# A hybrid encoder layer with routed experts: where the closing part loads its rows, and how the router's logits are multiplied

## What is computed

```python
def layer(...):
    h = rms_norm(x) * (1 + sc1) + sh1
    mix, ... = token_mixer(h, ...)            # gated short conv and windowed attention, merged, times w_mix_out
    x = x + g1 * mix                          # the kernel's "x2"
    h = rms_norm(x) * (1 + sc2) + sh2         # the kernel's "h2"
    top_idx, top_w = route(hf, w_router, router_bias)
    ffn = swiglu(hf, w_sh_gate, w_sh_up, w_sh_down) + routed_experts(hf, top_idx, top_w, ...)
    x = x + g2 * ffn
    return x                                  # then one last RMSNorm with a gain

def route(h, w_router, router_bias):
    scores = sigmoid(h @ w_router)            # (tokens, 64 experts), contraction over 1024
    # best 4 of 8 groups, best 8 experts in them, weights normalised and times 2.5
```

## Time and profile before

| | |
|---|---|
| median of the runs | 2250.11 us |
| profiled execution | 2247.8 us |
| its span | 2246.0 us |
| granted TensorE clock, mean | 0.979 of full speed |
| TensorE matmul busy | 2140.7 us (95%) |
| VectorE busy | 1230.8 us (55%) |
| ScalarE busy | 1007.1 us (45%) |
| GpSimd busy | 459.5 us (20%) |

### The profile page before, as it was taken

The page is one execution under the profiler, slowest core; times in us unless marked ns, Lnnn a source line. Parts: engine busy times, 40 slices in busy tenths (PEclk is TensorE's granted clock), DMA queues, the critical chain, the costliest instruction groups (busy, mean ns, idle before and its releaser), DMA issues. The chain is left out here.

```text
span 2246.0 us, 41415 instructions
## 1 busy us (share of the span) xinstructions
PE 2140.7 (95%) x11538; PEld 1834.9 (82%) x11539; DVE 1230.8 (55%) x2000; ACT 1007.1 (45%) x1773; POOL 459.5 (20%) x549
## 2 busy tenths in 40 slices
PE   5999899999999989998988999999999999999995
PEld 2767559999999989997878788888888888888862
DVE  4623673112332331215777787688677778678636
ACT  3403793211011121113432676677676677667622
POOL 1400000000000000000000444434444444434335
PEclk8999899999999999999999999999999999999998
DMA  7360501112111101116322899899889899989758
GB/s 294 125 241 9 177 1 56 38 47 66 47 47 40 34 19 47 47 52 233 115 64 86 295 326 312 252 304 335 278 285 340 279 325 309 312 253 324 253 133 244
DMA packets 153532, 395.59 MB, mean 176 GB/s; under 512 B 22124, under 2 KB 90932, under 8 KB 128900
## 3 DMA queue, kind: packets, MB, share of 16 engines
q1 hardware_dynamic: 122260, 311.61, 38.5%
q0 software_dynamic: 31040, 82.51, 14.9%
q10 hardware_dynamic: 176, 0.75, 0.1%
HBM read 353.93 MB, written 74.53 MB: 191 GB/s over the span
## 5 line engine op out<-in xcount | busy, mean ns | idle before, releaser
L2098 PE MATMUL ex_pgu<-ex_wgu_hi,ex_xT_hi 128*128 (+1 forms) x784 | 314.9, 402 | 9.9 <-DVE ex_xT_lo L2268 9.2
L2256 DVE TENSOR_TENSOR ex_wgu_lo<-ex_stage_gu,ex_wgu_hi (+1 forms) x252 | 291.8, 1221 | 37.2 <-ACT ex_wgu_hi L2175 37.0
L2098 PE MATMUL ex_pgu<-ex_wgu_hi,ex_xT_lo 128*128 (+1 forms) x784 | 308.1, 393 | 0.0
L2098 PE MATMUL ex_pgu<-ex_wgu_lo,ex_xT_hi 128*128 (+1 forms) x784 | 307.2, 392 | 0.0
L2175 ACT CAST ex_wgu_hi<-ex_stage_gu (+1 forms) x252 | 245.7, 1047 | 35.6 <-issue 18.7
L983 PE MATMUL cv_ph<-fourth_r,cv_split 128*128 128x352 f32 (+1 forms) x1152 | 222.0, 328 | 2.1 <-DVE cv_split L1029 2.1
L983 PEld LDWEIGHTS cv_ph<-fourth_r,cv_split 128*128 128x128 f32 x1152 | 196.0, 189 | 2.2 <-DVE cv_split L1029 2.2
L1624 POOL MEMSET ex_rows<- 128x1088 f32 x1 | 1.0, 1004 | 951.6 <-ACT third_r L1596 951.6
L2098 PEld LDWEIGHTS ex_pgu<-ex_wgu_hi,ex_xT_hi 128*128 128x128 f32 x784 | 148.4, 189 | 41.4 <-issue 11.8
L2098 PEld LDWEIGHTS ex_pgu<-ex_wgu_hi,ex_xT_lo 128*128 128x128 f32 x784 | 147.5, 188 | 31.4
L2098 PEld LDWEIGHTS ex_pgu<-ex_wgu_lo,ex_xT_hi 128*128 128x128 f32 x784 | 147.9, 189 | 28.7
(11 more groups left out here) (355 smaller groups left out, 4245.1 us busy)
## 6 DMA issues: line engine op xcount, KB each, us to landing
ex_stage_gu<-in_w_exp_gate SPq DMA_DIRECT2D x64, 1024.0 KB, 8.8
ex_stage_gu<-in_w_exp_up SPq DMA_DIRECT2D x64, 1024.0 KB, 11.7
ex_stage_dn<-in_w_exp_down SPq DMA_DIRECT2D x64, 1024.0 KB, 8.4
front_room<-in_w_ada SPq DMA_DIRECT2D x26, 512.0 KB, 5.8
w_ahead<-in_w_in SPq DMA_DIRECT2D x24, 512.0 KB, 3.8
third<-in_w_ada SPq DMA_DIRECT2D x16, 512.0 KB, 8.6
early_late<-in_w_in SPq DMA_DIRECT2D x16, 512.0 KB, 3.9
front_room<-in_w_in SPq DMA_DIRECT2D x3, 2048.0 KB, 12.6
```

Of the source, the lines that this page charges most:

```text
L2098: last = pe.matmul(pgu[:, :], xT[a][:, k, :], w, start=(k == 0 and (a, c) == PASSES[0]), stop=(k == KT - 1 and (a, c) == PASSES[-1]))
L2256: dve.tensor_tensor(gu_piece(1, slot, q), gu_raw(slot, q), gu_piece(0, slot, q).bitcast(F32), ALU.subtract).then_inc(gu_lo, 1)
```

## The change

In the closing part SP issues the eight `x2` rows one after the other, without waiting for `tail_sum`; it waits for the even scatters' own semaphore instead of `even_stored`, which is gone; and it loads the nine tiles of even sums with nothing between them.

The logits are multiplied the other way round: the router's 64 columns are the weights, the tokens are streamed. Contraction steps 0 to 3 add up in PSUM partitions 0 to 63, steps 4 to 7 in partitions 64 to 127, issued in turn. ScalarE copies the 128x128 result (experts of both halves by tokens) to SBUF, and one more matmul, with a matrix of two identities below each other (`both_halves`), adds the halves and turns them to tokens by experts. This last matmul stands in the next mix tile, behind its first two contraction steps.

```diff
-                        for k in range(KT):
-                            last = pe.matmul(pl[t % 2][:R, 0:NE], h2T[:, k, t * P:t * P + R], wr[:, k, :],
-                                             start=(k == 0), stop=(k == KT - 1))
-                        last.then_inc(lg, 1)
+                        for k in range(KT // 2):
+                            for a in range(2):
+                                j = a * (KT // 2) + k
+                                last = pe.matmul(pl[t % 2][a * NE:(a + 1) * NE, P:P + R], wr[:, j, :], h2T[:, j, t * P:t * P + R],
+                                                 start=(k == 0), stop=(k == KT // 2 - 1))
+                        last.then_inc(lg_halves, 1)
+
+                    def sum_halves(t):
+
+                        R = rows_of(t)
+                        pe.wait_ge(sum_ready, 1)
+                        pe.wait_ge(lg_out, t + 1)
+                        pe.matmul(pl[t % 2][:R, 0:NE], halves[t % 2][:, 0:R], both_halves, start=True, stop=True).then_inc(lg, 1)
...
+                            if k == 1 and t >= 3:
+                                sum_halves(t - 3)
...
+                                if half == 0 and k == 1 and q < 2:
+                                    sum_halves(NT - 2 + q)
...
                     logits(NT - 2)
+                    sum_halves(NT - 3)
                     unit(0)
...
+                    def halves_out(t):
+                        R = rows_of(t)
+                        act.wait_ge(lg_halves, t + 1)
+                        act.copy(halves[t % 2][:, 0:R], pl[t % 2][:, P:P + R]).then_inc(lg_out, 1)
...
                     for t in range(NT):
                         R = rows_of(t)
+                        if t >= 2:
+                            halves_out(t - 2)
                         act.wait_ge(x2_done, t + 1)
...
+                    dve.tensor_tensor(both_halves, con[:, C_ID:C_ID + NE], con[:, C_ID + NE:C_ID + P], ALU.add).then_inc(sum_ready, 1)
...
-                    AHEAD = 3
-                    for t in range(AHEAD):
+                    for t in range(NT - 1):
                         x2_rows(t)
-                    for t in range(AHEAD, AHEAD + 2):
-                        sp.wait_ge(tail_sum, t - AHEAD + 1)
-                        x2_rows(t)
-                    sp.wait_ge(even_stored, 1)
+                    sp.wait_ge(y_stored[0], pairs_of(sp) * 16 + 16)
                     for t in range(NT):
                         R = rows_of(t)
                         sp.dma_start(sums[t][:R, :], self.sum_rows[0][t * P:t * P + R, :]).then_inc(sum_loaded[t], 16)
-                        if AHEAD + 2 + t < NT - 1:
-                            x2_rows(AHEAD + 2 + t)
...
-                    wait(y_stored[0], m * 16 + 16)
-                    pool.sem_inc(even_stored, 1)
```

More of the change, by code:

```diff
@@ L1260, in mix_and_route @@
         sh_down_loaded = S("sh_w_down")
+        lg_halves, lg_out, sum_ready = map(S, ("mx_logit_halves", "mx_logit_halves_out", "mx_sum_of_halves"))
         sh_loaded, sh_prod, sh_sig, sh_gated, sh_done = map(S, ("sh_w", "sh_prod", "sh_sig", "sh_gated", "sh_done"))
@@ L1311, in mix_and_route @@
             wd = room(2, NE).rearrange("p (t n) -> p t n", n=NE)
+            both_halves = room(NE)
+            halves = [room(P), little(P)]
             wu_r = self.alias("sh_wu_r", [P, KT, DSH], F32R)
@@ L1596, in valued @@
                         act.activation(v, v.bitcast(F32), ACT.Copy, scale=con[:, C_VAL + t * TOPK:C_VAL + t * TOPK + 1]).then_inc(hot, 1)
+                    halves_out(NT - 2)
                     sigmoid(NT - 2)
@@ L1606, in _ @@
                     evac(NT - 1)
+                    halves_out(NT - 1)
                     sigmoid(NT - 1)
@@ L1835, in experts @@
         w_loaded = self.first_w
-        filled, ahead, even_stored = S("ex_filled"), S("cb_ahead"), S("cb_even_stored")
+        filled, ahead = S("ex_filled"), S("cb_ahead")
         x2_loaded = [S(f"cb_x2_{t}") for t in range(NT - 1)]
```

## The result

The changed kernel takes 2246.61 us (median of 20 runs, 2238.02 to 2251.25). The kernel before took 2249.68 in the 20 runs beside them (2246.11 to 2262.29). The ratio is 0.9977, with a 95% interval of 0.9967 to 0.9988: 0.2% faster, some 5 us, and not the forecast's 16. The profiled execution took 2238.02 us with a span of 2236.2, the shortest of its 20; a second profile of the same kernel has a span of 2246.3.

| stage | before | after | after, second profile |
|---|---|---|---|
| up to the first mix matmul | 1024.0 | 1019.4 | 1026.1 |
| mix tiles with the logits, up to the token count | 146.4 | 142.7 | 143.45 |
| up to the first closing matmul | 1002.6 | 1002.3 | 1004.4 |
| closing part | 73.0 | 71.7 | 72.3 |
| span | 2246.0 | 2236.2 | 2246.3 |

What follows compares the result with a forecast made beforehand. Bytes were taken to bound the closing part's middle and TensorE the merge stage; 13.0 us from the closing part and 2.9 from the logits, off 2250.1, gave 2234 us, range 2228 to 2243.

Steps and rivals of the forecast that it cites:

- The logits: Merge stage: 0.45 us less per tile, 2.7 us over six tiles plus 0.2 behind them, together 2.9 us, bounds -1.5 and 4.
- Start and bytes: Closing part: first even-sum load 8.4 us earlier, then 38.4 us of bytes; last odd tile lands 12.5 us earlier.
- GpSimd's first multiply: Closing part: 13.3 us earlier, behind the first even sum and its odd addition; 13 us taken as shift of all following GpSimd.
- The odd tile's addition: Closing part: the first addition of odd rows to an even sum, put at 9 us in full queues.
- The end: Closing part: VectorE ends behind GpSimd by the same 10.5 us as before, so the tail gains 13 us.
- the 8.19 us of the earlier trace: Closing part, kernel before: VectorE's L2326, 1.28 us alone, took this long at 2217.82 beside two back-to-back GpSimd multiplies.
- the second rival: Closing part: GpSimd keeps VectorE out, two tiles finished rather than five; gain 8 us, 2242 us; chance 0.13.
- The handover: Closing part, kernel before: VectorE got in between two GpSimd multiplies (3.35 us), so it wasn't taken as kept out throughout.
- The first rival: Closing part: TensorE becomes the tail's floor; gain 18.4 us there plus 2.9, 2229 us; chance 0.20.

Runs made afterwards that it cites:

- the turns: The changed kernel, but GpSimd's multiply of tile t waits until VectorE has finished the output of tile t-3: 2231.93 us, ratio 0.9914 to the kernel before.
- in order: The changed kernel, but in the logits all matmuls of one half come before all of the other's: 2251.62 us, ratio 0.9993 to the kernel before.
- the fills: The changed kernel without the multiply by g2; GpSimd fills a buffer twice in place of each multiply (result not the layer's): 2232.51 us, one run.
- one engine for both: The changed kernel, but VectorE makes the multiply by g2 itself and GpSimd only starts transfers: 2231.69 us, ratio 0.9907 to the kernel before.

## Why the prediction was wrong

**The logits: right in the sum, in part by luck.** A tile's logits take 1.02 us (forecast 1.05), the sum of the halves 0.14 (0.21). The stretch is shorter by 2.4 to 3.8 us in pairs of profiles that differ in this part alone or with the turns (146.4 and 146.5 without it, 142.7 to 144.1 with it); the term was 2.9. But it had 0.45 us a tile and 2.7 us before the last mix tile's end, and 0.2 behind it. Measured, the period shrank by 0.27 to 0.30, six times 1.7 us, and the rest came behind the last mix tile: from its last matmul to the token count it is 0.9 to 1.5 us less. Each tile loses some 0.27 us beside the logits: in the tile from 1082.21 the eight transposes take 0.96 us for 0.87 and the 48 mix matmuls 11.20 for 11.02. The Trainium skill, TensorEngine Tiling (Array Packing), section Tiling Modes, says that tiles run matmuls in parallel and that a change of mode drains the engine. The first half agrees, 1.02 us alternating against 1.51 in order; no run here measured the drain by itself. If the 0.27 us are its price, it ate half of the gain and not all; that isn't shown.

**Start and bytes: right, but for one wait.** The even scatter's data let the first sum load go 5.3 us after the scatter's issue, and 8.5 us earlier in the closing part (forecast 8.4). The moved `x2` rows cost nothing: the last landed at 2164.31, 2.6 us before that load, where 6 were forecast. GpSimd's first multiply came 18.8 us after the closing part's start, where it had been 29.25: 10.4 us earlier, 2.9 less than the 13.3 forecast. The odd tile's addition, put at 9 us, took 8.75. What was missing is the wait for the last odd scatter: the forecast let the addition start when the first even sum was there (2170.39), and it started at 2174.45, behind the scatter's landing at 2173.82. The nine loads that the change put beside this scatter made it last 7.2 us instead of 2.7, and it does so in each of the seven profiles with the moved loads (6.7 to 7.5). GpSimd's end came 15.0 us earlier all the same (44.1 us after the closing part's start, 59.1 before), 2 more than forecast. The forecast counted 1.5 us of waiting in GpSimd's 29.8 us; there were 3.0, in four places, and its last multiply lost 1.0 to VectorE (3.35 us for 2.35). In the changed kernel all that is gone, and the chain takes 25.3 us.

**The end: the step that failed.** It read: "with VectorE behind GpSimd by the same 10.5 us, the tail gains 13". Measured, VectorE ended 24.3 us behind GpSimd (2208.54 to 2232.79). The 13.8 us between the two took back all but 1.3 of GpSimd's 15. The distance of 10.5 us was no constant: it stood for four tiles of 2.58 us left over (with the same closing code and the logits changed it is 8.0). Now eight are left over, which is 10.3 us more, and another 3.3 us are VectorE's waits for TensorE at tiles 7 and 8: TensorE had stood still behind the held instruction, and from 2210.98 on its last tiles are on the chain that ended last. Before, VectorE got a turn at five of GpSimd's nine multiplies, most of them where GpSimd waited for rows that hadn't come. VectorE in the kernel before, ahead of the 8.19 us of the earlier trace rows:
```profile
2210.20 2.88 DVE L2326 SCALAR_TENSOR_TENSOR cb_room<-cb_room,cb_ri,ex_stage_dn 128x1024 f32<-128x1024 f32 x1
...
2214.38 2.14 DVE L2326 SCALAR_TENSOR_TENSOR cb_room<-cb_room,cb_ri,ex_stage_dn 128x1024 f32<-128x1024 f32 x1
```
These two waited under 2 us each until a multiply ended; GpSimd's next work, the start of a later tile's transfer, began only 0.17 and 0.74 us after that end, as the even rows for it had landed no sooner (2211.87 and 2215.88). The 8.19 us fell where three multiplies came without such a pause. By loading the rows earlier the forecast took GpSimd's waits away, and it kept the turns that VectorE had had beside them.

I had this mechanism as the second rival, at 0.13, and priced it too low: two tiles finished in place of five and 8 us of gain left. It was one in place of five, and 1.3 us, which is within what the closing part differs between two profiles of the same code. I held against it that "the waits for the last odd tiles remain"; they don't, as GpSimd's last wait is the one before 2183.28, and the rows of the last two tiles had landed at 2200.82 and 2202.75, before their multiplies. The handover that I relied on the earlier trace rows was real: at 2228.80, between two multiplies without a pause, VectorE got in, and in the run with the logits alone it did so three times more. But it is no rule that holds in the changed kernel, where VectorE lost at six multiplies in a row. The Trainium skill, SBUF — State Buffer, section Who interferes with whom (on the shared port pair), had the rule to follow: an exclusive lock, the loser blocks fully, and a write-only GpSimd instruction doesn't take part. All three agree: 19.38 us, and 1.28 beside the fills. Who gets in next is a question of its own (below).

The runs bear this out from two sides. Take away the overlap of the two readers (turns, or one engine for both) and the closing part is 58.6 or 57.8 us; from the old 73.0 that is 14.4 and 15.2 less, about the 13 forecast. Keep the overlap and move only the loads, and it is 72.8. The first rival, TensorE as the tail's floor, didn't decide: it had 13.36 us of idle time, and was late at the end by that.

**Still open.** What spreads the time up to the first mix matmul by 7.7 us. What the 0.27 us beside each tile's logits are. And the rule of the handover. In the six profiles without turns in which GpSimd multiplies, a pattern holds at every multiply's end at which VectorE was waiting and GpSimd had another multiply to make: VectorE got in where GpSimd's next instruction, multiply or transfer start, was recorded no more than 0.07 us before that end (9 times), and was kept out where it was recorded 0.37 us or more before it (27 times). With turns it got in each time, in two cases with a transfer start recorded 0.68 and 1.02 us before, but there the next multiply was held back by the semaphore. No run varied this lead by itself, so it is a pattern and no cause shown.

## What to carry to other kernels

When a change removes waits on one engine, ask who used them: here VectorE had most of its turns beside GpSimd's waits, none once GpSimd had nothing to wait for, and a gain of 15 us upstream came to 1.3 or nothing at the end. Where a GpSimd instruction and a VectorE one both read two operands from SBUF, count them one after the other, and if one queue is always ready, give the other its turn by a semaphore or put both on one engine. Loads that are moved earlier meet other transfers there: look what else lands in that stretch, and who waits for it. An engine's distance behind another is a sum of its own: work it out anew from tiles left over, and don't carry it across the change.

## What the runs showed of the hardware

- A `scalar_tensor_tensor` of 1.28 us was held for 18.1 us across seven multiplies of GpSimd and three starts of transfers between them. The order was not by age: it waited from 2190.25, and six multiplies that started later went first. The length was 19.37 or 19.38 us in four profiles.
- The same instruction was let in between back-to-back multiplies, after a wait of 0.7 us, where GpSimd's next multiply was recorded only 0.03 to 0.05 us before the end of the one in front (2.0 us instead of 1.28, three times in the run with the logits alone).
- Taking turns costs little: each of the two waits for the other, 2.28 us for 1.28 and 0.41 to 1.23 us of idle time, and a tile takes 3.58 us, against 3.85 on VectorE alone.
- Float32 matmuls with 64 columns of weights overlapped best when neighbours in the queue used different halves: 1.02 us for 16 alternating, 1.51 in order, 1.71 with the operands exchanged. The transposes and mix matmuls around them took 0.27 us more a tile.
- A scatter of 144 packets of under 512 B took 2.7 us in empty queues and 7.2 beside nine loads of 128 or 64 rows.
- After 13.36 us of idle time TensorE's granted clock was at its lower level (0.51 from 2200 to 2208, 0.50 from 2208 to 2211), and eight matmuls took 5.12 us instead of 3.59.
